# A hybrid decoder trunk on one core: low parts in pieces, a softplus of two steps, and an earlier place for output and k low steps

## The reference, cut to what matters

```
z = q k^T * 64**-0.5                       # strictly causal
log_keep = log_sigmoid(-z) = -softplus(z)  # 0 where masked
between = sum of log_keep over the later keys
a = exp(log_sigmoid(z) + between)
o = a v
```

## Time and profile before

| | |
|---|---|
| three runs | 1576.17, 1576.52, 1578.27 us; median 1576.52 |
| the profiled execution | 1578.2 us; span in the trace 1576.4 us |
| PE busy | 1520.6 us, 96% of the span |
| DVE, ACT, POOL busy | 921.2, 648.2, 607.0 us |
| stages | attention to about 283 us, MLP to 675, embedding to 735, retention to 1145, MLP to 1503, embedding to the end |

### The profile page before, as it was taken

The page is one execution under the profiler, slowest core; times in us unless marked ns, Lnnn a source line. Parts: engine busy times, 40 slices in busy tenths (PEclk is TensorE's granted clock), DMA queues, the critical chain, the costliest instruction groups (busy, mean ns, idle before and its releaser), DMA issues. The chain is left out here.

```text
span 1576.4 us, 19898 instructions
## 1 busy us (share of the span) xinstructions
PE 1520.6 (96%) x6874; PEld 1256.3 (80%) x6874; DVE 921.2 (58%) x1217; ACT 648.2 (41%) x1035; POOL 607.0 (39%) x242
## 2 busy tenths in 40 slices
PE   8898998999999999998999999999999999999996
PEld 5777787878888888876888888888878888888874
DVE  6777878877777731157443352433777777730155
ACT  6687777433232322234353342432533232322232
POOL 3223222444444444443434334243344444444440
PEclk9999999999999999999999999999999999999998
DMA  4111101222222332223213222132222222232221
GB/s 157 54 54 53 53 36 58 88 92 101 93 93 100 104 121 104 78 80 120 94 54 108 80 80 101 59 106 80 80 83 104 93 93 98 104 122 101 81 80 54
DMA packets 37193, 137.78 MB, mean 87 GB/s; under 512 B 4128, under 2 KB 4256, under 8 KB 37024
## 3 DMA queue, kind: packets, MB, share of 16 engines
q1 hardware_dynamic: 36576, 134.61, 24.2%
q10 hardware_dynamic: 576, 2.62, 0.4%
HBM read 135.12 MB, written 2.10 MB: 87 GB/s over the span
## 5 line engine op out<-in xcount | busy, mean ns | idle before, releaser
L307 POOL TENSOR_TENSOR wl<-raw,wh 128x1024 fp32r<-128x1024 f32 (+1 forms) x236 | 604.9, 2567 | 934.6 <-ACT wh L1090 934.5
L335 PE MATMUL bank<-xh,wh 128*128 128x512 f32 x1280 | 503.5, 393 | 7.9 <-DVE xl L725 7.8
L339 PE MATMUL bank<-xh,wl 128*128 128x512 f32 x1280 | 500.5, 391 | 0.0
L338 PE MATMUL bank<-xl,wh 128*128 128x512 f32 x1280 | 500.5, 391 | 0.0
L1090 ACT ACTIVATE wh<-raw 128x1024 fp32r<-128x1024 f32 (+1 forms) x236 | 258.8, 1099 | 439.7 <-PE bank L335 389.3
L335 PEld LDWEIGHTS bank<-xh,wh 128*128 128x128 f32 x1280 | 241.8, 189 | 60.0 <-DVE xl L725 10.5
L339 PEld LDWEIGHTS bank<-xh,wl 128*128 128x128 f32 x1280 | 241.5, 189 | 50.8
L338 PEld LDWEIGHTS bank<-xl,wh 128*128 128x128 f32 x1280 | 241.8, 189 | 49.5 <-issue 0.2
L739 DVE TENSOR_TENSOR x<-x,bank 128x512 f32<-128x512 f32 x56 | 38.4, 685 | 233.1 <-PE bank L339 233.0
L903 DVE SCALAR_TENSOR_TENSOR conv<-gate,par,conv 128x512 f32<-128x512 f32 x88 | 153.6, 1746 | 13.2 <-DVE conv L899 5.0
L335 PE MATMUL bank<-yh,wh 128*128 128x512 f32 x352 | 136.9, 389 | 0.0
(11 more groups left out here) (174 smaller groups left out, 1959.7 us busy)
## 6 DMA issues: line engine op xcount, KB each, us to landing
raw<-in_w SPq DMA_DIRECT2D x204, 512.0 KB, 3.2
raw<-in_w SPq DMA_DIRECT2D x32, 704.0 KB, 4.0
x<-in_xT SPq DMA_DIRECT2D x8, 256.0 KB, 5.1
outT<-x SPq DMA_DIRECT2D x8, 256.0 KB, 2.1
pin<-in_pT ACTq DMA_DIRECT2D x2, 512.0 KB, 4.8
decay<-in_consts ACTq DMA_DIRECT2D x1, 1024.0 KB, 5.8
rotary<-in_consts ACTq DMA_DIRECT2D x1, 512.0 KB, 3.7
cst<-in_consts SPq DMA_DIRECT2D x1, 256.0 KB, 7.2
```

What stands on the lines that cost most here:

```text
L307: nc.gpsimd.tensor_tensor(wl[:, slot, cols], raw_slot(ATT_RING if like < ATT_TILES else RAW_RING, r, blocks), wh[:, slot, cols].bitcast(F3 ...
L335: first = mm(out, ah_, bh_, start=start, stop=False, skip_group_check=True)
L338: mm(out, ah_, bl_, start=False, stop=False, skip_group_check=True)
L339: return mm(out, al_, bh_, start=False, stop=stop, skip_group_check=True)
```

## The change

- POOL's subtraction of a tile is done in instructions of two blocks (256 columns): four in place of one for a tile of 8 blocks, six for one of 11. The count goes up with the last.
- Softplus is Ln(1 + Exp(z)) on ACT, and DVE takes max(z, min(that, 20)) in place of max(z, 0) + ln. Abs is gone. Exp of bank jj waits for the low part of the same jj of the head before, not for all four.
- The two blocks of both_h and both_l lie inside sph[2] and spl[2], which are 512 columns wide now: columns 0 to 127 hold the first block as it is, columns 256 to 383 the sum. ACT's two copies and the semaphore are gone; PE reads the two blocks with a stride of 256 columns.
- DVE's `take_o` stands behind `take_qk`, ahead of the low parts of `al`. In half 1, `take_qk_low` (k) also stands ahead of all four `al`.
- Scores of half 0 wait for three of the four `qk_low` steps of their pair, those of half 1 for the fourth.

```diff
+SOFTPLUS_LINEAR = 20.0
+LOW_BLOCKS = 2
...
-            both_h, both_l = sb("both_h", [2, P], F32R, ph), sb("both_l", [2, P], F32R, ph)
+            both_h, both_l = sph[TB - 2][:, 2 * P:3 * P], spl[TB - 2][:, 2 * P:3 * P]
...
+                for b in range(0, blocks, LOW_BLOCKS):
+                    cols = slice(b * P, min(b + LOW_BLOCKS, blocks) * P)
+                    last = nc.gpsimd.tensor_tensor(wl[:, slot, cols], part[:, cols], wh[:, slot, cols].bitcast(F32),
+                                                   ALU.subtract)
+                last.then_inc(w_low, 1)
...
-                    pe.wait_ge(qk_low, 4 * p + 4)
+                pe.wait_ge(qk_low, 4 * p + 3 + half)
...
-                        pe.wait_ge(both_copied, 2 * s + 2)
...
+                            out = out.rearrange("p (a t) -> p a t", t=P)
+                            parts = [part[j2][:].rearrange("p (a t) -> p a t", t=2 * P)[:, :, 0:P] for part in (sph, spl)]
...
-                    vec.scalar_tensor_tensor(sp[j][:], Z[j][:, 0:T - j * P], 0.0, sp[j][:], ALU.max, ALU.add)\
+                    vec.scalar_tensor_tensor(sp[j][:], sp[j][:], SOFTPLUS_LINEAR, Z[j][:, 0:T - j * P], ALU.min, ALU.max)\
...
-                for jj in range(1, TB):
-                    weights_low(jj - 1)
-                    if more and jj == 1:
+                if not first:
+                    take_o(s - 1, p - (1 - half), 1 - half)
+                if more and half == 1:
+                    take_qk_low(p + 1, half, 1 - par_)
+                for jj in range(TB):
+                    weights_low(jj)
+                    if more and half == 0 and jj == 0:
                         take_qk_low(p + 1, half, 1 - par_)
-                weights_low(TB - 1)
                 if more and half == 1:
                     take_v(p + 1)
-                if not first:
-                    take_o(s - 1, p - (1 - half), 1 - half)
...
-                    nc.scalar.activation(sp[j][:], Z[j][:, 0:T - j * P], ACT.Abs).then_inc(z_abs, 1)
...
+                    if not first:
+                        act.wait_ge(a_low, 4 * s - 4 + jj + 1)
                     act.wait_ge(z_done, 4 * s + jj + 1)
+                    nc.scalar.activation(sp[j][:], Z[j][:, 0:T - j * P], ACT.Exp).then_inc(z_exp, 1)
...
-                if not first:
-                    act.wait_ge(a_low, 4 * s)
...
-                act.wait_ge(sp_low, 4 * s + 2)
-                for both_, part in ((both_h, sph), (both_l, spl)):
-                    copy(both_[:, 0, :], part[TB - 2][:, 0:P].bitcast(F32), both_copied)
```

More of the change, by code:

```diff
@@ L131, in program @@
             sp = [sb(f"sp{j}", [T - j * P], F32, ph) for j in range(TB)]
-            sph = [sb(f"sph{j}", [T - j * P], F32R, ph) for j in range(TB)]
-            spl = [sb(f"spl{j}", [T - j * P], F32R, ph) for j in range(TB)]
+            sph = [sb(f"sph{j}", [T if j == TB - 2 else T - j * P], F32R, ph) for j in range(TB)]
+            spl = [sb(f"spl{j}", [T if j == TB - 2 else T - j * P], F32R, ph) for j in range(TB)]
             both = sb("both", [P], F32, ph)
-            both_h, both_l = sb("both_h", [2, P], F32R, ph), sb("both_l", [2, P], F32R, ph)
+            both_h, both_l = sph[TB - 2][:, 2 * P:3 * P], spl[TB - 2][:, 2 * P:3 * P]
             ah = [sb(f"ah{j}", [T - j * P], F32R, ph) for j in range(TB)]
@@ L189, in program @@
         q_zeros = sem("q_zeros")
-        z_done, z_abs, z_exp, z_ln = sem("z_done"), sem("z_abs"), sem("z_exp"), sem("z_ln")
+        z_done, z_exp, z_ln = sem("z_done"), sem("z_exp"), sem("z_ln")
         sp_full, sp_high, sp_low = sem("sp_full"), sem("sp_high"), sem("sp_low")
-        both_full, both_high, both_low, both_copied = (
-            sem(n) for n in ("both_full", "both_high", "both_low", "both_copied"))
+        both_full, both_high, both_low = (sem(n) for n in ("both_full", "both_high", "both_low"))
         cum_done, a_full, a_high, a_low = sem("cum_done"), sem("a_full"), sem("a_high"), sem("a_low")
@@ L304, in split_low @@
                 slot, r, blocks, _, _ = place(like)
-                cols = slice(0, blocks * P)
+                part = raw_slot(ATT_RING if like < ATT_TILES else RAW_RING, r, blocks)
                 pool.wait_ge(w_high, n + 1)
-                nc.gpsimd.tensor_tensor(wl[:, slot, cols], raw_slot(ATT_RING if like < ATT_TILES else RAW_RING, r, blocks),
-                                        wh[:, slot, cols].bitcast(F32), ALU.subtract).then_inc(w_low, 1)
+                for b in range(0, blocks, LOW_BLOCKS):
[3 more added lines that the diff above has]
+                last.then_inc(w_low, 1)
             for head in range(2):
@@ L405, in cumulate @@
                         pe.wait_ge(both_low, s + 1)
-                        pe.wait_ge(both_copied, 2 * s + 2)
                     for j2 in range(j, TB if j == TB - 2 else max(j + 1, TB - 1)):
                         left = negtri if j2 == j else negones
-                        parts = (sph[j2][:], spl[j2][:])
+                        out = Z[j][:, (j2 - j) * P:T - j * P]
+                        parts = (sph[j2][:, 0:T - j2 * P], spl[j2][:, 0:T - j2 * P])
                         if j < j2 == TB - 2:
-                            parts = (both_h[:].rearrange("p a t -> p (a t)"), both_l[:].rearrange("p a t -> p (a t)"))
+                            out = out.rearrange("p (a t) -> p a t", t=P)
+                            parts = [part[j2][:].rearrange("p (a t) -> p a t", t=2 * P)[:, :, 0:P] for part in (sph, spl)]
                         for part in parts:
-                            last = mm(Z[j][:, (j2 - j) * P:T - j * P], left[:], part, start=False,
-                                      stop=True, skip_group_check=True)
+                            last = mm(out, left[:], part, start=False, stop=True, skip_group_check=True)
                     last.then_inc(cum_done, 1)
@@ L822, in softplus_high @@
                     dve.wait_ge(sp_full, 4 * s + jj + 1)
-                    vec.tensor_copy(sph[j][:], sp[j][:]).then_inc(sp_high, 1)
+                    vec.tensor_copy(sph[j][:, 0:T - j * P], sp[j][:]).then_inc(sp_high, 1)
                 def softplus_low(jj):
@@ L827, in softplus_low @@
                     dve.wait_ge(sp_high, 4 * s + jj + 1)
-                    low(spl[j][:], sp[j][:], sph[j][:], sp_low)
+                    cols = slice(0, T - j * P)
+                    low(spl[j][:, cols], sp[j][:], sph[j][:, cols], sp_low)
                 def last_two():
@@ L833, in last_two @@
                     dve.wait_ge(both_full, s + 1)
-                    vec.tensor_copy(both_h[:, 1, :], both[:]).then_inc(both_high, 1)
+                    vec.tensor_copy(both_h, both[:]).then_inc(both_high, 1)
                     dve.wait_ge(both_high, s + 1)
-                    low(both_l[:, 1, :], both[:], both_h[:, 1, :], both_low)
+                    low(both_l, both[:], both_h, both_low)
                 def weights_low(jj):
@@ L1165, in slot, with exponential @@
                 s = 2 * p + half
-                def magnitude(jj):
+                def exponential(jj):
                     j = TB - 1 - jj
+                    if not first:
+                        act.wait_ge(a_low, 4 * s - 4 + jj + 1)
                     act.wait_ge(z_done, 4 * s + jj + 1)
-                    nc.scalar.activation(sp[j][:], Z[j][:, 0:T - j * P], ACT.Abs).then_inc(z_abs, 1)
[L1172 to L1175, removed]
+                    nc.scalar.activation(sp[j][:], Z[j][:, 0:T - j * P], ACT.Exp).then_inc(z_exp, 1)
                 def ln_one_plus(jj):
@@ L1180, in ln_one_plus @@
                     nc.scalar.activation(sp[j][:], sp[j][:], ACT.Ln, bias=1.0).then_inc(z_ln, 1)
-                if not first:
-                    act.wait_ge(a_low, 4 * s)
[L1184 to L1188, removed]
-                act.wait_ge(sp_low, 4 * s + 2)
-                for both_, part in ((both_h, sph), (both_l, spl)):
-                    copy(both_[:, 0, :], part[TB - 2][:, 0:P].bitcast(F32), both_copied)
+                for t in range(TB + 1):
+                    if t < TB:
+                        exponential(t)
+                    if t:
+                        ln_one_plus(t - 1)
                 if not first:
```

## The result

The changed kernel takes 1552.69 us (median of four runs, 1551.37 to 1555.96) against 1577.13: a ratio of 0.985, interval [0.9837, 0.9863]. The profiled execution is the slowest of the four, 1555.96, with a span of 1554.2 and a mean granted clock of 0.992 (0.995 to 0.996 in the other three); against the earlier trace rows's execution it is 22.2 us shorter.

The account below looks back on a forecast made before the run. PE, busy 96% of the span, was taken as the bound, so only its idle 56 us could be won. Terms 12.8 + 1.4 + 1.4 - 1.0 = 14.6 off 1576.5 gave 1562 us, range 1554 to 1573.

Parts of the forecast that it names:

- the steps that would be blocked in each half: DVE in a pair: blocked by 7 of POOL's 12 pieces, 1.4 us in half 0, 1.9 and 2.0 in half 1.
- the new wait at the values: In a pair, PE would wait about 1.1 us at the values, for al jj = 3.
- A piece of 256 columns is then 0.55 + 0.20 = 0.75 us: POOL's instruction: column part plus fixed part, 0.75 us, also the most a lone DVE step waits.
- 24.1: DVE's time in us for a pair after the change, own work 22.7 plus idle 1.4, before POOL's blocks.
- DVE was to stand idle for 1.4 us a pair: DVE's idle time left in a pair: gaps between dependent steps and a short wait for Ln.
- pairs 1 to 6 repeat each other within 0.1 us: Reading of the kernel before: pairs of heads 1 to 6 nearly alike, each holding 2.65 us of PE slack.
- 1.4 for the retention's start: Retention's start, PE's waits for xl: pieces bring xl sooner, sumsq_l only 0.5; 1.4 us gained (0 to 3).
- a sign of being wrong: PE waiting for w_low, POOL's low parts, was named as showing the forecast wrong.
- so I cost it at 0; with the cover gone it would be 0.6 us a tile: POOL's tiles in pieces: w_low comes 0.6 us later, charged at 0 since PE never waits for it.
- take_o fills the wait and costs nothing: DVE in a pair: take_o, 2.0 us, moved into the 2.27 wait before al; chain starts up to 2 us sooner.
- (a): Rival: PE sets the pace in the pairs, blocks stay near 3 us; gain about 22, 1554 us; chance 0.23.
- (c): Rival: slower, POOL's pieces take the port before DVE's steps in every pair; 1584 us; chance 0.08.

Follow-up runs that it names:

- e12: The changed kernel with pieces of two blocks in the attention alone and whole tiles from there on: 1558.93 us, ratio 0.989.
- e9: The changed kernel with the first 12 weight tiles behind the attention in one POOL instruction each: 1553.00 us, ratio 0.985.
- e3: The kernel before with only the new order on DVE and the finer qk_low count: 1581.16 us, ratio 1.0027.
- e2: The changed kernel with POOL's low parts in one instruction a tile again: 1581.24 us, ratio 1.0032.
- e4: The kernel before with only softplus in two steps, no ACT copies and the finer a_low count: 1595.12 us, ratio 1.0119.
- e7: The changed kernel with POOL pieces of one block (128 columns): 1543.80 us, ratio 0.9796.
- e8: The changed kernel with POOL pieces of four blocks (512 columns): 1563.83 us, ratio 0.9916.
- e5: The kernel before with pieces, the new DVE order and the finer qk_low count, softplus as before: 1575.03 us, ratio 0.9988.
- O: The part with the order on DVE and the finer count of qk_low; alone on the kernel before: 1581.16 us, ratio 1.0027.
- S: The part with softplus in two steps, without ACT's copies, and the finer a_low count; alone on the kernel before: 1595.12 us, ratio 1.0119.
- e6: The kernel before with pieces, two-step softplus and the finer a_low count, order on DVE as before: 1568.98 us, ratio 0.9944.
- P: The part with POOL's low parts in pieces of two blocks; alone on the kernel before: 1570.68 us, ratio 0.9961.

## Why the prediction was wrong

**Right.** The bound (only PE's idle time counts, none of it in the MLP's windows), the turns (one DVE step, one piece), nearly all of the steps that would be blocked in each half (three instead of two in half 0, one k part instead of both in half 1), the new wait at the values, DVE as what paces a pair, and the sign.

**The term that failed is the piece: "A piece of 256 columns is then 0.55 + 0.20 = 0.75 us"**, charged as the block of each of 7 steps, 5.3 us a pair. A piece does last that long on POOL (0.72 to 0.75 us undisturbed). What failed is taking this length for what a blocked DVE step loses. It loses the column part alone: in one pair 9 steps lose 3.9 us (0.44, 0.53, 0.42 in half 0; 0.28, 0.53, 0.42, 0.52, 0.33, 0.43 in half 1). That alone would make 24.1 + 3.9 = 28.0 us in place of 29.4. Measured is 28.7, since a second term was too small: DVE was to stand idle for 1.4 us a pair and does for 2.4, some 1.0 of it waiting for Ln in half 1 (its own work is 22.4 instead of 22.7: 22.4 + 3.9 + 2.4 = 28.7). PE has 0.75 us of waits left instead of 1.1. The mechanism stood. The loss of a blocked step was forecast at almost twice its size, and the error in the idle time, the other way, hid 1.0 of it; that a pair came out within 0.7 us is partly luck. Stage by stage, in the two profiled executions:

| stretch | forecast | measured |
|---|---|---|
| start to first scores | 1.4 | 2.15 |
| pairs 0 to 6 | 11.6 | 16.7 |
| last pair and residual phase | 1.0 | -1.3 |
| MLP of layer 0 | 0 | -2.2 |
| embedding and retention's start | 1.1 | 5.6 |
| the rest | -0.5 | 1.2 |

The pairs are short of the measured gain by 5.1 us and the retention's start by 4.5, and the two stages that got longer hide 4.5 of this.

**Two terms are of PE's clock**, which the sum had none for. It was there to be seen: the sentence that pairs 1 to 6 repeat each other within 0.1 us holds for pairs 1 to 4 alone (30.9). Pair 5 of the kernel before takes 31.65 at a mean clock of 0.95, and pair 6 30.10. Windows of PE (busy, granted clock, DMA share, GB/s), the kernel before at the retention's start and the changed kernel behind the residual phase:

```profile
740.00:742.00 2.00, 0.35 (x1) 0.65 0.97 406
742.00:744.00 2.00, 2.00 (x6) 0.50 1.02 410
744.00:746.00 2.00, 2.00 (x6) 0.50 0.05 21
```

```profile
300.00:302.00 2.00, 0.96 (x3) 0.90 0.00 0
302.00:304.00 2.00, 0.83 (x2) 0.50 0.22 31
304.00:306.00 2.00, 2.00 (x6) 0.50 0.62 231
306.00:308.00 2.00, 2.00 (x6) 0.50 0.01 4
```

In both PE stood still twice in a short time: 3.16 and 1.80 us before, 1.40 and 2.17 after. By the windows' mean clock (0.65 and 0.90) it fell within the second stop, at about 740.6 and 301.6 us, and PE then ran at 1.2 instead of 2.4 GHz, 6 matmuls in 2 us where 10 or 11 are usual. In the first place the stops shrank from 4.96 to 1.65 us in sum, and the slow stretch went with them: 3.3 us of stops and 2.3 that is left, 5.6 us where I had 1.4 for the retention's start. e12, which brings the stops back, has the slow stretch again. In the second one it appeared, and is the whole 2.2 us that the MLP's stage is longer: e9, with one stop of 0.81 there, has none, and its stage takes 367.1 us against 369.6. This term belongs to the profiled execution. The three others, 2.7 to 4.6 us shorter at a higher mean clock, probably lack it, but they left no trace; that would be the 2.2 us by which the gain of the medians, 24.4, exceeds the profiled one.

That stops bring the slow stretch is what these places agree on; it was not tried by itself, and no rule comes out of it. A stop of 1.70 us at 269 us of the kernel before was followed by 3.4 us at the lower clock. Of the seven pairs, with stops for spl of 1.9 us one has a slow stretch in the kernel before and three in e3, with 2.4 four (e2), with 2.4 to 2.5 six (e4), and with 1.3 or less none (the changed kernel, e7, e8); but e5, whose pairs hold a stop of 1.9 for al, has none either. So part of what pieces are worth to O and S may be the clock; e5 and e6, whose pairs are all at full clock, still show that the parts do not add up.

**"so I cost it at 0; with the cover gone it would be 0.6 us a tile"** was wrong for the start and the residual phase: I looked at PE's waits, and the ring there closes over SP, the load and ACT. PE waits 2.5 us for w_low, which the prediction had named as a sign of being wrong. **"take_o fills the wait and costs nothing"** was right for the whole change and wrong as a reason: e3 and e5 show that the filled gap only moves until softplus is shortened. Summed part by part (O, S, P) the change would be +4.5, +18.5 and -6 us; the forecast was as near as it is because the pair was placed as a whole.

Of the rivals (a), PE as the pace, came closest in time, 1554, but for another cause: the pieces did not lose their turns, DVE still paces the pair in the changed kernel, and e7 is what comes near (a). The range did not take in (a) whole, as the prediction says: 1554 is (a)'s own middle, so that its faster half lay outside, and with it the measured time. Its gain adds up to 22.9, not 22. (c) is real, under another name: it is what softplus alone does with whole tiles.

**The Trainium skill** (SBUF — State Buffer, Who interferes with whom) says that the pair is held for the whole instruction and that the other engine fully blocks. The turns bear it out. The price does not follow from it: a blocked step loses 2.1 ns a column from 128 to 1024 columns, and none of the 0.2 us that an instruction takes besides. With the measured 0.45 us of a piece of one block, the page's sentence gives an estimate of 0.45 us a step; measured are 0.15 to 0.26.

## What to carry to other kernels

Where two engines take turns at a resource, price a step by what it is measured to lose to the other, not by the length of the other's instruction, and measure that with two sizes before any sum. A gap that another engine's latency leaves is not free room: if a step moves into it, look at which latency the step covered in its old place. And parts of a change that are each slower alone may pay only together, so place the whole period and don't add up the parts. Before any of it, look at the granted clock of each period: a longer period can be the same work at the lower clock.

## What the runs showed of the hardware

- A POOL subtraction is recorded with 0.45 us for 128 columns (eight in a row take 3.4) and 2.39 for 1024, and a DVE step with two SBUF inputs, or a cast between SBUF tiles, loses 2.1 ns a column to it: 0.15 to 0.26 us for 128 columns, 2.04 to 2.16 for 1024.
- DVE and POOL alternate when both wait, one instruction each: with pieces of 256 columns three xl steps at the retention's start take 3.51 us instead of 6.28.
- PE's granted clock fell to half within the second of two stops (3.16 and 1.80 us; 1.40 and 2.17) and behind one of 1.70; with 1.65 us in four stops it did not. Stops of 1.9 us in a pair brought it in one of seven pairs in the kernel before, in three of seven in e3.
